# One core, two transformer blocks in float32: where the inner tiles of the FFN are split into high and low part

## The reference

```python
def swiglu(h, w_gate, w_up, w_down):
    return (jax.nn.silu(h @ w_gate) * (h @ w_up)) @ w_down
...
        h = rms_norm(x, norm_ffn_pre[layer])
        f = swiglu(h, w_ffn_gate[layer], w_ffn_up[layer], w_ffn_down[layer])
        x = x + rms_norm(f, norm_ffn_post[layer]).astype(x.dtype)
```

## Time and profile before

| | |
|---|---|
| median of 3 executions | 2701.59 us (2701.45 to 2701.74) |
| the profiled execution | 2701.17 us |
| its span, first to last instruction | 2699.4 us |
| TensorE matmuls busy | 2686.2 us, 16180 instructions |
| VectorE busy | 1815.3 us, 2603 instructions |
| ScalarE busy | 1293.7 us, 1942 instructions |
| GpSimd busy | 57.0 us |
| TensorE's granted clock, mean | 0.999 of 2.4 GHz |

### The profile page before, as it was taken

The page is one execution under the profiler, slowest core; times in us unless marked ns, Lnnn a source line. Parts: engine busy times, 40 slices in busy tenths (PEclk is TensorE's granted clock), DMA queues, the critical chain, the costliest instruction groups (busy, mean ns, idle before and its releaser), DMA issues.

```text
span 2699.4 us, 40708 instructions
## 1 busy us (share of the span) xinstructions
PE 2686.2 (100%) x16180; PEld 2365.8 (88%) x16180; DVE 1815.3 (67%) x2603; ACT 1293.7 (48%) x1942; POOL 57.0 (2%) x59
## 2 busy tenths in 40 slices
PE   9999999999999999999999999999999999999998
PEld 7887888899988888788889998999988877899987
DVE  6944655588854784555568884588854798688843
ACT  5334533455542533643455563365542457555631
POOL 0030000000000003000000000000000000000000
PEclk9999999999999999999999999999999999999999
DMA  4241233233332224133323333233332330233332
GB/s 149 79 128 64 90 97 102 82 118 102 101 101 89 86 79 133 51 98 101 101 84 110 113 93 99 82 117 102 97 105 88 117 114 2 71 118 108 95 102 80
DMA packets 80219, 259.63 MB, mean 96 GB/s; under 512 B 9936, under 2 KB 12368, under 8 KB 79536
## 3 DMA queue, kind: packets, MB, share of 16 engines
q1 hardware_dynamic: 74160, 248.57, 29.3%
q10 hardware_dynamic: 5888, 8.68, 1.2%
HBM read 247.51 MB, written 2.10 MB: 92 GB/s over the span
## 4 chain that ended last, share of the span: by engine, by line
PE 98%; DVE 1%; ACT 1%; issue 0%; ACTq 0%; POOL 0%; DVEq 0%; POOLq 0%
PE bank L484 30%; PE bank L485 30%; PE bank L486 30%; PE bank L1878 1%; PE bank L1856 1%; PE bank L1637 1%; PE bank L1842 1%; PE bank L1653 1%; PE bank L1684 1%; PE bank L1774 0%; PE bank L1665 0%; PE bank L551 0%; PE bank L559 0%; DVE x L836 0%; PE bank L1668 0%
## 5 line engine op out<-in xcount | busy, mean ns | idle before, releaser
L484 PE MATMUL bank<-u_hi,w_hi 128*128 128x512 f32 (+1 forms) x2352 | 799.5, 340 | 0.9 <-DVE w_lo L670 0.9
L485 PE MATMUL bank<-u_lo,w_hi 128*128 128x512 f32 (+1 forms) x2352 | 790.1, 336 | 0.0
L486 PE MATMUL bank<-u_hi,w_lo 128*128 128x512 f32 (+1 forms) x2352 | 789.8, 336 | 0.0
L670 DVE TENSOR_TENSOR w_lo<-raw,w_hi 128x1024 fp32r<-128x1024 f32 x346 | 426.6, 1235 | 450.2 <-ACT w_hi L666 448.4
L666 ACT ACTIVATE w_hi<-raw 128x1024 fp32r<-128x1024 f32 x346 | 364.2, 1054 | 335.8 <-PE bank L486 283.5
L484 PEld LDWEIGHTS bank<-u_hi,w_hi 128*128 128x128 f32 x2352 | 446.6, 190 | 51.9 <-DVE w_lo L670 3.2
L485 PEld LDWEIGHTS bank<-u_lo,w_hi 128*128 128x128 f32 x2352 | 446.6, 190 | 47.2 <-issue 2.4
L486 PEld LDWEIGHTS bank<-u_hi,w_lo 128*128 128x128 f32 x2352 | 446.5, 190 | 46.1
L484 PE MATMUL bank<-cm,w_hi 128*128 128x256 f32 x1152 | 326.0, 283 | 0.0
L485 PE MATMUL bank<-cm,w_hi 128*128 128x256 f32 x1152 | 326.0, 283 | 0.0
L486 PE MATMUL bank<-cm,w_lo 128*128 128x256 f32 x1152 | 326.0, 283 | 0.0
(11 more groups left out here) (319 smaller groups left out, 3602.2 us busy)
## 6 DMA issues: line engine op xcount, KB each, us to landing
raw<-in_weights SPq DMA_DIRECT2D x338, 512.0 KB, 3.4
rx<-in_weights SPq DMA_DIRECT2D x72, 512.0 KB, 3.4
raw<-in_weights SPq DMA_DIRECT2D x48, 256.0 KB, 2.7
raw<-in_weights SPq DMA_DIRECT2D x32, 384.0 KB, 3.0
rot_s<-rot_in ACTq DMA_DIRECT2D x32, 128.0 KB, 2.3
q_s<-q_in ACTq DMA_DIRECT2D x52, 64.0 KB, 2.9
x<-in_x SPq DMA_DIRECT2D x4, 512.0 KB, 6.5
ret_mask<-in_ret_mask SPq DMA_DIRECT2D x2, 1024.0 KB, 6.3
```

The source lines that it names most:

```text
L484: nc.tensor.matmul(out, st_hi, mv_hi, start=first, stop=False, skip_group_check=onto)
L485: nc.tensor.matmul(out, st_hi, mv_lo, start=False, stop=False, skip_group_check=onto)
L486: return nc.tensor.matmul(out, st_lo, mv_hi, start=False, stop=last, skip_group_check=onto)
L670: nc.vector.tensor_tensor(w_lo[:, bl.slot(p), :], raw[:, bl.raw(p), :], w_hi[:, bl.slot(p), :].bitcast(F32), ALU.subtract).then_inc(lo_spl ...
```

## The change

All hidden splits are taken out of the last turn. On ScalarE tile 4 is split behind the turn and ahead of `silu_right`, tiles 5, 6 and 7 between `silu_right` and `silu_21`, and the other eighteen behind `silu_21`. On VectorE `hidden_right` and `gate_21` come first, then the first fourteen of `CONVERT` (4 to 13, 2, 3, 0, 1), then `up_21`, then tiles 14 to 21. The order of the tiles, `CONVERT`, `FIRST_DOWN` and everything on TensorE and on the queue of SyncE stay. The diff, cut to its core:

```diff
             for j in range(ST):
-                before, end = j > 0, j == ST - 1
+                before = j > 0
                 split_ahead(j, 3)
                 fork_a(j, BY_GATE)
                 if before:
                     silu_right(j - 1)
-                if end:
-                    hidden_high(4)
                 split_ahead(j, 4)
                 fork_a(j, BY_UP)
                 if before:
                     silu_21(j - 1)
-                if end:
-                    hidden_high(5)
                 fork_p5(j, BY_GATE)
                 split_ahead(j, 5)
                 fork_p5(j, BY_UP)
-                if end:
-                    hidden_high(6)
-                    hidden_high(7)
                 fork_u2(j, BY_GATE)
                 split_ahead(j, 6)
                 fork_u2(j, BY_UP)
-                if end:
-                    hidden_high(8)
-                    hidden_high(9)
                 split_ahead(j, 7)
                 silu_11(j)
-                if end:
-                    hidden_high(10)
-                    hidden_high(11)
                 fork_u3(j, BY_GATE)
                 split_ahead(j, 8)
                 fork_u3(j, BY_UP)
-                if end:
-                    hidden_high(12)
-                    hidden_high(13)
                 split_ahead(j, 9)
-            for k in (2, 3, 0, 1):
-                hidden_high(k)
+            hidden_high(CONVERT[0])
             silu_right(ST - 1)
-            for k in range(14, 18):
+            for k in CONVERT[1:4]:
                 hidden_high(k)
             silu_21(ST - 1)
-            for k in range(18, FT):
+            for k in CONVERT[4:]:
                 hidden_high(k)
...
-                if end:
-                    hidden_low(4)
                 sum_t(j)
...
-                if end:
-                    hidden_low(12)
-                    hidden_low(13)
                 split_ahead(j, 9)
                 scale_right(j)
                 add_u2(j, BY_UP)
-            for k in (2, 3, 0, 1):
-                hidden_low(k)
             hidden_right(ST - 1)
             gate_21(ST - 1)
-            for k in range(14, 18):
+            for k in CONVERT[:14]:
                 hidden_low(k)
             up_21(ST - 1)
-            for k in range(18, FT):
+            for k in range(14, FT):
                 hidden_low(k)
```

More of the change, by code:

```diff
@@ L1354, in dve_ffn @@
                     up_21(j - 1)
-                if end:
-                    hidden_low(5)
                 split_ahead(j, 5)
-                if end:
-                    hidden_low(6)
-                    hidden_low(7)
                 split_ahead(j, 6)
                 gate_11(j)
-                if end:
-                    hidden_low(8)
-                    hidden_low(9)
                 split_ahead(j, 7)
-                if not end:
+                if j + 1 < ST:
                     sum_weights(j + 1)
                 up_11(j)
-                if end:
-                    hidden_low(10)
-                    hidden_low(11)
                 split_ahead(j, 8)
```

## The result

The changed kernel takes 2728.48 us in the median (2726.31 to 2729.25, four executions) against 2701.66 us (2701.45 to 2701.78) on the same chip: ratio 1.0098, interval 1.0086 to 1.0111. That is 26.8 us slower; 25.6 were forecast (2727.2 us, range 2722 to 2736). The profiled execution is the fastest of the four, 2726.31 us with a span of 2724.5, so it shows 25.1 us of the loss.

The account below looks back on a forecast made before the run. TensorE's back-to-back matmuls were taken as the bound, leaving next to nothing to gain. Two stalls, 6.0 us per FFN or 24.0 for four, plus 1.6 for the clock, gave 25.6 us: 2727.2 us, range 2722 to 2736.

Parts of the forecast that it names:

- Bound, and no gain inside the turn: Last Strassen turn: TensorE is never held there, so removing the hidden splits gains 0; the turn stays 20.16 us.
- The 8.4 us of which I said that VectorE is freed in the last turn: VectorE's queue in the last turn: fourteen low parts of 0.60 us leave it, saving 8.4 us.
- the rival that is not slower: VectorE, freed in the last turn, runs ahead and has tile 4 ready in time: 2700.7 to 2701.6 us, chance 0.02.
- First stall 2.7 us: Start of the down projection: TensorE waits for tile 4's low part behind hidden_right and gate_21, 2.7 us per FFN.
- Second stall 3.3 us, from the eleventh place of tile 2: Fifth down tile: TensorE takes tile 2 but VectorE splits it eleventh, a 3.3 us wait per FFN.
- the sign to look for: Profile after: eight TensorE waits on hid_lo low parts, four of 2.7 and four of 3.3 us.
- The queue behind: Splits of down blocks 3 and 4 behind the low parts: not late, 5.5 us distance; rival 2731 to 2739, chance 0.07.
- The clock: TensorE's clock may fall at the stalls: 1.6 us taken, one fall in four FFNs; rival 2732 to 2736.4, chance 0.25.
- the tail's 2.7 us: End of the kernel: the clock falls about 2.7 us after TensorE's last matmul, taken as the mark for stalls.
- The 10.8 us that I gave for it at worst: Upper bound of the clock term: every second stall brings the clock down, 4 x 2.7 us.

Follow-up runs that it names:

- ahead: Changed kernel with its fourteen splits behind the turn but ahead of silu_right, hidden_right and gate_21: 2728.17 us, loss 26.5.
- four_in: Changed kernel with tiles 4 to 7 split inside the last turn again, order of splits unchanged: 2723.81 us, loss 22.1.
- order: Changed kernel with CONVERT as 4, 5, 6, 7, 2, 3, 0, 1, 8 to 21, so tile 2 is split fifth: 2718.02 us, loss 16.7.
- ahead_order: Changed kernel with fourteen splits behind the turn but ahead of the right half, and tile 2 split fifth in CONVERT: 2710.84 us, loss 9.2.
- fill_first: Changed kernel with 11 idle matmuls ahead of the wait for tile 4 only: 2732.81 us, loss 31.4.
- again: The changed kernel, unaltered, measured once more: 2729.01 us, loss 27.6.
- fill: Changed kernel with idle matmuls into a free bank, 11 ahead of tile 4 and 13 ahead of tile 2: 2726.93 us, loss 25.6.
- fill_second: Changed kernel with 13 idle matmuls ahead of the wait for tile 2 only: 2730.35 us, loss 28.9.
- order_fill: Changed kernel with tile 2 split fifth in CONVERT and 11 idle matmuls ahead of tile 4: 2713.25 us, loss 11.9.

## Why the prediction held, point by point

- **Bound, and no gain inside the turn.** Shown: the turn is 20.16 us with and without the hidden tiles, and VectorE gave back 0.46 us there, of which 0.36 go in the wait for the silu. The 8.4 us of which I said that VectorE is freed in the last turn are 10 x 0.60 = 6.0 us; the other four of the fourteen low parts stood behind the turn before. No term of the sum uses the figure; the rival that is not slower does, and it did not come true.
- **First stall 2.7 us.** The wait in the list is 2.68 us in all four FFNs, but from start to start tile 4 is 2.84 us late, where 2.72 were forecast. I had counted 0.05 us from the end of the low part to the matmul, from a release between VectorE and ScalarE; here it is 0.15 (755.08 to 755.23). This has no part in the total, since the second stall ends when VectorE gets to tile 2. Its two causes are told apart by ahead (1.3 us remain with the right half behind the tiles) and four_in (0 remain with tiles 4 to 7 in the turn).
- **Second stall 3.3 us, from the eleventh place of tile 2.** The delay of tile 2 is 6.03 us against 6.0 forecast, and order removes the second stall. The waits themselves read 0.5 to 1.5 us in the first profiled execution (3.0 in two FFNs of the second), not the 3.3 that I gave as the sign to look for: I had worked out that four tiles at half rate would end ahead of tile 2, but didn't carry it into the signs.
- **The queue behind.** It isn't late in the changed kernel (the split of block 3 starts at 767.97 where 767.5 + 0.4 was forecast). It is in ahead_order, 0.5 us, by the path through ScalarE, which the prediction followed as far as high part 21 and not to the table load and the split behind it.
- **The clock.** This is the term that was worked out wrongly, though its size came near. I took the tail's 2.7 us as the mark, with the first stalls below it and the second ones a little above, and counted one fall in four FFNs, at 1.6 us. The runs show a fall in every FFN in both traces of the changed kernel, most of them by the first stall, and a price that depends on where it comes: nothing between the stalls, 1.4 us by the second. The second stall brought the clock down in two FFNs of eight, those whose first stall had not; fill_first, where no first stall can do so, has it in four of four. The costly falls are thus as many as I took, one FFN in four, but not for my reason, and the two traces have none and two: 0.1 us and 2.8 us for the clock. That 1.6 lies between them, and near the 2.1 of again minus fill, is in good part luck. The rule of the Trainium skill ("TensorE: Matmul & The Clock Gate", section "Why this matters for your kernels"), that idle gaps between bursts bring the clock back to half rate, was right for these stalls: the traces agree with a fall in all eight FFNs. The 10.8 us that I gave for it at worst did not come, because the second stall covers the falls of the first.
- **The slow restart** was not in the sum: 0.13 us per FFN behind tile 2, 0.5 us.

By terms, in the two profiled executions of the changed kernel: 24.1 us to the start of tile 2, 0.5 for the restart there, 0.1 and 2.8 for the clock, 0.4 and 0.6 ahead of the first FFN. These are 25.1 and 28.0 us; the spans are 25.1 and 28.1 us longer than the 2699.4 of the kernel before.

## What to carry to other kernels

In a kernel whose TensorE never waits, work on another engine can be moved behind a stage only as far as the first tiles that the next stage takes are still ready; list them in the order of their consumer and count from there. The first four here cost 2.8 us per FFN and a wrong place in a list 3.2, while the other ten cost 0.1. A stall of TensorE of 2.7 us or more had a second price in the clock here, and whether it is paid depends on what stands behind it: removing one of two stalls, or filling it with idle work, can give back less than its length or nothing.

## What the runs showed of the hardware

- Counted in the traces above: behind a stall of 1.3 us (ahead_order, and the first stalls of ahead) the clock fell in 0 of 8 cases. Behind a lone 2.7 us (order, fill_second) it fell in 7 of 8, behind a lone 3.0 to 3.5 us (the second stalls of fill_first and ahead, and four_in) in 12 of 12. The first stalls of the changed kernel, 2.7 us too, brought it down in 4 of 4 FFNs in one trace and 2 of 4 in the other.
- A fall lasted 3.4 us in most cases and 6.8 us in two, and its start came between 1.2 us ahead of the restart and 1.3 us behind it, differently from FFN to FFN and from execution to execution. That makes 2.7 of the 3 us between the two profiled executions of the changed kernel. With the idle matmuls of order_fill the spread is 0.3 us, against 2.3 in order; in fill, where the profiled execution has no fall either, it is 1.1.
- Idle matmuls into a free bank hold the clock at its upper level, but they are worth it only where nothing else absorbs the fall: 4.8 us won in order_fill, 4 us lost in fill_first.
- The first matmul behind a wait, or with its operand only just there, took 0.30 to 0.34 us to the next start instead of 0.23 with the clock up, and 0.56 to 0.59 instead of 0.43 where it was down by then.
